# The opening of a three-block network on one core: four modulation groups as direct matmuls

## The reference, cut to what matters

```
mod = silu(c) @ ada_w[0] + ada_b[0]          # c: 1024, ada_w[0]: 1024 x 9216
sh1, sc1, g1, ... = split(mod, 9)            # 1024 each
h = rms_norm(x) * norm_g * (1 + sc1) + sh1   # the first layer's norm
x = x + 0.5 * g1 * swiglu(h, ff_w13, ff_w2)
...
m = rms_norm(mem, norm_mem_2[i])             # i = 0, 1: 256 memory tokens
mk, mv = split(m @ w_mem_kv_2[i], 2)         # 256 columns of keys, 256 of values
mk = rms_norm over each head of 64           # (inside the attention)
```

## Time and profile before

| | |
|---|---|
| median of 3 runs | 3224.15 us (3220.56 to 3226.03) |
| profiled execution | 3219.94 us, its span 3218.1 us |
| mean granted clock of TensorE | 0.968 |
| busy: TensorE, VectorE, ScalarE | 95%, 72%, 53% |
| the opening (up to the `wide` step) | 0 to 87.3 us |

### The profile page before, as it was taken

The page is one execution under the profiler, slowest core; times in us unless marked ns, Lnnn a source line. Parts: engine busy times, 40 slices in busy tenths (PEclk is TensorE's granted clock), DMA queues, the critical chain, the costliest instruction groups (busy, mean ns, idle before and its releaser), DMA issues.

```text
span 3218.1 us, 48507 instructions
## 1 busy us (share of the span) xinstructions
PE 3061.1 (95%) x20774; PEld 2819.0 (88%) x20774; DVE 2316.6 (72%) x2612; ACT 1700.4 (53%) x1902; POOL 84.2 (3%) x163
## 2 busy tenths in 40 slices
PE   5999899999988999899979999999999999889999
PEld 5999799999988998799968888888887888889999
DVE  6786668788555556655575888898898888646575
ACT  3434443443534335443535777777777777445453
POOL 1010001011000000000000000000000000000000
PEclk9999899999989999999988999999999999989999
DMA  7685458688421653245413999999999999423353
GB/s 278 248 309 213 151 192 295 234 292 309 158 73 66 223 205 130 79 157 184 158 40 120 365 349 343 366 355 350 351 349 363 341 358 363 166 103 134 116 187 118
DMA packets 112316, 739.27 MB, mean 230 GB/s; under 512 B 12480, under 2 KB 12480, under 8 KB 32096
## 3 DMA queue, kind: packets, MB, share of 16 engines
q1 hardware_dynamic: 89424, 651.21, 54.3%
q0 software_dynamic: 22672, 84.91, 7.4%
HBM read 735.01 MB, written 1.05 MB: 229 GB/s over the span
## 4 chain that ended last, share of the span: by engine, by line
PE 74%; DVE 8%; ACT 3%; DMA 2%; issue 1%; DVEq 0%; ACTq 0%; POOLq 0%
PE ps L521 54%; PE ps L520 18%; DVE wlo L2701 3%; PE ps L530 2%; DMA ring<-in_w 2%; DVE AF L2683 2%; ACT whi L1814 2%; DVE att L2692 0%; DVE gf L2686 0%; DVE AF L2674 0%; DVE hl L2674 0%; ACT cv L1802 0%; DVE gs L2689 0%; DVE T L2674 0%; DVE X L2674 0%
## 5 line engine op out<-in xcount | busy, mean ns | idle before, releaser
L2701 DVE TENSOR_TENSOR wlo<-ring,whi 128x2048 fp32r<-128x2048 f32 x620 | 1416.6, 2290 | 444.3 <-ACT whi L1814 443.4
L1814 ACT ACTIVATE whi<-ring 128x2048 fp32r<-128x2048 f32 x620 | 1185.0, 1914 | 350.9 <-issue 202.3
L521 PE MATMUL ps<-whi,AR 128*128 128x512 f32 (+1 forms) x2724 | 881.2, 398 | 0.7 <-DVE AR L2674 0.4
L521 PE MATMUL ps<-hh,whi 128*128 128x256 f32 x2464 | 696.3, 283 | 4.0 <-DVE wlo L2701 3.6
L521 PE MATMUL ps<-hl,whi 128*128 128x256 f32 x2464 | 689.4, 280 | 0.0
L521 PE MATMUL ps<-hh,wlo 128*128 128x256 f32 x2464 | 688.9, 280 | 0.0
L521 PEld LDWEIGHTS ps<-whi,AR 128*128 128x128 f32 x2724 | 511.0, 188 | 116.1 <-DVE AF L2674 1.1
L521 PE MATMUL ps<-wlo,AR 128*128 128x512 f32 (+1 forms) x1362 | 535.2, 393 | 0.0
L521 PEld LDWEIGHTS ps<-hh,whi 128*128 128x128 f32 x2464 | 463.6, 188 | 9.4 <-DVE wlo L2701 3.8
L521 PEld LDWEIGHTS ps<-hl,whi 128*128 128x128 f32 x2464 | 463.5, 188 | 1.2 <-issue 1.0
L521 PEld LDWEIGHTS ps<-hh,wlo 128*128 128x128 f32 x2464 | 463.2, 188 | 0.3
(11 more groups left out here) (234 smaller groups left out, 3238.1 us busy)
## 6 DMA issues: line engine op xcount, KB each, us to landing
ring<-in_w SPq DMA_DIRECT2D x620, 1024.0 KB, 5.2
rring<-in_r POOLq DMA_DIRECT2D x151, 512.0 KB, 5.0
AF<-in_mem POOLq DMA_DIRECT2D x2, 1024.0 KB, 5.9
X<-in_x POOLq DMA_DIRECT2D x1, 1024.0 KB, 13.6
AF<-in_cst POOLq DMA_DIRECT2D x1, 1024.0 KB, 5.7
y_out<-X SPq DMA_DIRECT2D x1, 1024.0 KB, 3.9
cst<-in_cst POOLq DMA_DIRECT2D x1, 672.5 KB, 4.7
sm<-in_small POOLq DMA_DIRECT2D x1, 378.0 KB, 4.9
```

Source lines behind the costliest of these rows:

```text
L521: return self.e.matmul(out, l, r, start=start, stop=stop)
L1814: self.e.activation(N.whi[:, c % HB, :], N.ring[:, c % RING, :], ACT.Copy).then_inc(N.sem["hi"], 1)
L2701: self.e.tensor_tensor(N.wlo[:, c % HB, :], N.ring[:, c % RING, :], N.whi[:, c % HB, :].bitcast(F32), ALU.subtract).then_inc(N.sem["lo"], 1)
```

## The change

- TensorE's new `direct(g, q)` multiplies a raw chunk by `ca`: the weights are its 128x128 blocks, the moving operand one column, 8 calls a chunk, and the four columns of a group add up in PSUM. `HEAD` gives the order: groups 2, 3, 0, 1. VectorE only adds the bias (`ada_sums` for g < 4, `part_sums`).
- The memory's norm factor is no longer multiplied in ahead of the products. `upper` and `lower` work on the memory as it was loaded (`s_xm`), with the gain only. The values get the factor as the scale of their copy out of PSUM (`copy_nat`), and the key norm takes care of it by a bias of 1e-6 times the memory's mean square plus 1e-6 squared (`ms`, `key_root`), since the keys are normed again. The memory's `spread` goes.
- The second memory has tiles of its own (`s_mh2`, `s_ml2`), so `hh` and `hl` are free, and the first layer's norm is applied inside `memory`.
- Loads: GpSimd issues small, three raw chunks, mem, cst, x, where it was cst, small, mem, three raw chunks, x. SP waits for x, not for mem, and sends weight chunks 1, 2 and 3 only when raw chunks 5, 8 and 11 have been used.
- The engines' orders in `memory` are rewritten: on TensorE eight raw chunks, both stats, four, the spread, four, then both layers' keys, then the values; `start` of TensorE and VectorE doesn't wait for cst, and ScalarE makes its small tables later (`tables`).

```diff
         assert ar.n <= free
+        ar = Arena(self.AR)
+        self.s_ml2, self.s_mh2 = ar.take(8, S), ar.take(8, S)
...
-                (self.scale if (key, "n") == FIRST else self.norm)((key, "n"), self.N.X, ("mod", l, 2 * j))
+                if (key, "n") != FIRST:
+                    self.norm((key, "n"), self.N.X, ("mod", l, 2 * j))
...
+HEAD = [(g, q) for g in (2, 3, 0, 1) for q in range(4)]
...
     def start(self):
-        self.wait_ge("ld_cst", 16)
-        self.wait_ge("ld_small", 16)
         self.wait_ge("dve", "ones")
         self.wait_ge("act", "consts")
...
+    def direct(self, g, q):
+
+        l, j = divmod(g, 18)
+        b = self.take(("ada", g)) if q == 0 else self.ps(("ada", g))
+        i, c = self.raw([(0, "ada_w", (l,), q * 256, 2, (j * 512, 512))])
+        for k in range(2):
+            w = self.N.ca[:, 2 * q + k:2 * q + k + 1]
+            for m in range(4):
+                o = k * 512 + m * P
+                t = self.mm(b[:, m:m + 1], c[:, o:o + P], w, q == 0 and k == 0 and m == 0, q == 3 and k == 1, skip=True)
+        t.then_inc(*self.up(("raw", i), *([("ada", g)] if q == 3 else [])))
+
     def memory(self):
 
 
         N = self.N
         self.base, self.span = 0, 7
-        for g in range(4):
-            self.ada(g, 0)
-            self.ada(g, 1)
         self.adan = 4
+        for g, q in HEAD[:8]:
+            self.direct(g, q)
         self.stat("mem", [N.s_tm[:, k, :] for k in range(8)])
-        self.spread("mem")
         self.stat(FIRST, [N.T[:, k, :] for k in range(8)])
+        for g, q in HEAD[8:12]:
+            self.direct(g, q)
+        self.wait_ge("ld_cst", 16)
+        self.wait_ge("act", "tables")
         self.spread(FIRST, 7)
-        self.ada_sums(0)
-
-        def lin(i, hh, hl):
+        for g, q in HEAD[12:]:
+            self.direct(g, q)
+        halves = ((N.s_mh, N.s_ml), (N.s_mh2, N.s_ml2))
+        for i, (hh, hl) in enumerate(halves):
             self.lin(("mem", i, "k"), [(0, "w_mem_kv_2", (i,), 0, 8, (0, 256))], ("mem", i), hh=hh, hl=hl)
-
-        def nat(i, hh, hl):
-            self.lin_nat(("mem", i, "v"), [(0, "w_mem_kv_2", (i,), 0, 8, (256, 256))], ("mem", i), hh=hh, hl=hl)
-
-        lin(0, N.s_mh, N.s_ml)
-        nat(0, N.s_mh, N.s_ml)
         self.pair_stat("mk0")
-        self.ada_sums(1)
-        lin(1, N.hh, N.hl)
+        nats = [self.nat_steps(("mem", i, "v"), [(0, "w_mem_kv_2", (i,), 0, 8, (256, 256))], ("mem", i), hh=hh, hl=hl)
+                for i, (hh, hl) in enumerate(halves)]
+        next(nats[0])
         self.pair_rows("mk0")
-        nat(1, N.hh, N.hl)
-        self.mark(("mem", 1, "in"))
+        self.pair_stat("mk1")
+        next(nats[0])
         self.pair_bcast("mk0")
-        self.ada_sums(2)
-        self.pair_stat("mk1")
-        self.ada_sums(3)
         self.pair_rows("mk1")
+        next(nats[1])
         self.pair_bcast("mk1")
+        next(nats[1])
+        self.mark(("stfree", self.row["mem"]))
...
     def start(self):
         N = self.N
+        self.wait_ge("dve", "ones")
+        self.act(N.misc[:, 62:63], N.ones[:, 0:1], ACT.Silu)
+        self.wait_ge("ld_small", 16)
+        self.act(N.ca[:, :], N.V("c", 0), ACT.Silu, "consts")
+        self.loaded = self.here()
+
+    def tables(self):
+        N = self.N
         self.wait_ge("ld_cst", 16)
         self.act(N.identb[:, :], N.C("ident"), ACT.Copy)
         self.act(N.maskb[:, :], N.C("mask"), ACT.Copy)
-        self.act(N.warm[:, :], N.C("iota")[:, 0:P], ACT.Copy)
-        self.wait_ge("ld_small", 16)
-        self.act(N.ca[:, :], N.V("c", 0), ACT.Silu, "consts")
-        self.wait_ge("act", "consts")
+        self.act(N.warm[:, :], N.C("iota")[:, 0:P], ACT.Copy, "tables")
 
     loaded = 0
...
-    def copy_nat(self, key, dst, wid=256):
+    def copy_nat(self, key, dst, wid=256, scale=None):
         for tb in range(2):
             self.wait_ge("mm", (key, tb))
-            self.act(dst(tb), self.ps((key, tb))[:, 0:wid], ACT.Copy, (*key, tb), ("free", (key, tb)))
+            kw = {} if scale is None else {"scale": scale[:, tb:tb + 1]}
+            self.act(dst(tb), self.ps((key, tb))[:, 0:wid], ACT.Copy, (*key, tb), ("free", (key, tb)), **kw)
 
...
     def memory(self):
         N = self.N
         self.adan = 4
-        self.squares("mem", N.s_xm, 8, lambda k: self.wait_ge("ld_mem", 16), N.s_tm)
-        self.squares(FIRST, N.X, 8, lambda k: self.wait_ge("ld_x", 16), N.T)
-        self.root("mem", 1024)
+        ms = N.misc[:, 34:36]
 
         def upper(i, hh):
             gain = N.V("norm_mem_2", i)
             for k in range(8):
-                self.wait_ge("dve", ("mem", "z", k))
-                self.act(hh[:, k, :], N.s_tm[:, k, :], ACT.Copy, (("mem", i), "hi", k), scale=gain[:, k:k + 1])
+                self.act(hh[:, k, :], N.s_xm[:, k, :], ACT.Copy, (("mem", i), "hi", k), scale=gain[:, k:k + 1])
 
         def keys(i):
             self.copy_out(("mem", i, "k"), N.m_mk[i])
             self.pair_squares(f"mk{i}", N.m_mk[i], "act", ("mem", i, "k"))
-            self.copy_nat(("mem", i, "v"), lambda tb: N.m_mv[i][:, tb, :])
-
-        self.split_to(1)
+
+        def key_root(i):
+            key = f"mk{i}"
+            st = N.st[:, self.take_row(key), :]
+            self.wait_ge("mm", (key, "ss"))
+            ss = self.ps((key, "ss"))
+            self.act(st[:, 0:4], ss[:, 0:4], ACT.Sqrt, scale=1.0 / 64, bias=ms[:, 0:1])
+            self.act(st[:, 4:8], ss[:, 4:8], ACT.Sqrt, (key, "sqrt"), ("free", (key, "ss")), scale=1.0 / 64, bias=ms[:, 1:2])
+
+        def values(i):
+            self.wait_ge("dve", ("mem", "rstd"))
+            self.copy_nat(("mem", i, "v"), lambda tb: N.m_mv[i][:, tb, :], scale=N.st[:, self.row["mem"], :])
+
+        self.wait_ge("ld_mem", 16)
         upper(0, N.s_mh)
+        self.squares("mem", N.s_xm, 8, lambda k: None, N.s_tm)
+        self.squares(FIRST, N.X, 8, lambda k: self.wait_ge("ld_x", 16), N.T)
+        self.tables()
+        self.wait_ge("mm", ("mem", "ss"))
+        self.act(ms, self.ps(("mem", "ss"))[:, 0:2], ACT.Identity, ("mem", "ms"), scale=EPS / 1024, bias=N.C("eps2"))
+        self.root("mem", 1024)
+        self.split_to(0)
         self.root(FIRST, 1024)
-        upper(1, N.hh)
+        upper(1, N.s_mh2)
+        self.split_to(2)
+        self.wait_ge("dve", ("part", 0, 0))
+        self.halves(FIRST, N.T, N.hh, 8, gain_of(N, ("mod", 0, 0))[1])
         self.split_to(3)
+        self.wait_ge("act", ("mem", "ms"))
         keys(0)
-        self.root("mk0", 64, 4)
+        self.split_to(4)
+        keys(1)
+        key_root(0)
         self.rows_out("mk0", 4)
         self.split_to(5)
-        keys(1)
-        self.root("mk1", 64, 4)
+        key_root(1)
         self.rows_out("mk1", 4)
-        self.wait_ge("mm", ("mem", 1, "in"))
+        values(0)
+        values(1)
...
         self.e.memset(self.N.rT[1][:, :], 0.0).then_inc(*self.up("zeros"))
-        self.wait_ge("ld_cst", 16)
         self.wait_ge("ld_small", 16)
...
             if k >= 2:
                 self.lower(key, N.T, N.hl, N.hh, (k - 2,), shift)
-        if key == FIRST:
-            self.pair("mk1", N.m_mk[1], N.V("g_mk_2", 1))
 
...
         cols = N.mod[:, l, m]
+        if g < 4:
+            self.tt(cols, self.ps(("ada", g))[:, 0:4], N.V("ada_b", l)[:, m], ALU.add, ("free", ("ada", g)))
+            if j % 2:
+                self.part_sums(l, part)
+            return
         turned = self.ps(("ada", g)).rearrange("p (a b) -> p a b", a=4)
         self.e.tensor_reduce(out=cols, in_=turned, axis=AX, op=ALU.add).then_inc(*self.up(("free", ("ada", g))))
         self.wait_ge("dve", self.here())
         self.tt(cols, cols, N.V("ada_b", l)[:, m], ALU.add)
         if j % 2:
-            self.wait_ge("dve", self.here())
-            mm = N.mod[:, l, part * 8:part * 8 + 8]
-            if part % 3 == 1:
-                self.stt(N.gain[:, l, part // 3, :], mm, 1.0, N.V("norm_g", l, part // 3), ALU.add, ALU.mult)
-            elif part in (2, 8):
-                self.ts(mm, mm, 0.5, None, ALU.mult, None)
-            self.mark(("part", l, part))
+            self.part_sums(l, part)
+
+    def part_sums(self, l, part):
+        N = self.N
+        self.wait_ge("dve", self.here())
+        mm = N.mod[:, l, part * 8:part * 8 + 8]
+        if part % 3 == 1:
+            self.stt(N.gain[:, l, part // 3, :], mm, 1.0, N.V("norm_g", l, part // 3), ALU.add, ALU.mult)
+        elif part in (2, 8):
+            self.ts(mm, mm, 0.5, None, ALU.mult, None)
+        self.mark(("part", l, part))
 
...
             gain = N.V("norm_mem_2", i)
             for k in range(8):
                 self.wait_ge("act", (("mem", i), "hi", k))
-                self.stt(hl[:, k, :], N.s_tm[:, k, :], gain[:, k:k + 1], hh[:, k, :].bitcast(F32), ALU.mult, ALU.subtract,
+                self.stt(hl[:, k, :], N.s_xm[:, k, :], gain[:, k:k + 1], hh[:, k, :].bitcast(F32), ALU.mult, ALU.subtract,
                          (("mem", i), "h", k))
 
```

(54 more changed lines are left out.)

## The result

The changed kernel takes 3242.41 us (median of 5 runs, 3238.38 to 3244.24), the kernel before 3220.56 in the same rounds: ratio 1.0064 [1.0049 to 1.0078], so 0.64% slower. The forecast was 3247, 3242.7 for the profiled execution; that one took 3242.41 around a span of 3240.6, which is 22.5 longer than before, where 22.8 were forecast. The 3247 was 22.8 on top of 3224.15, the median of the kernel before over three runs; its median over all five is 3220.56, and that difference of 3.6 is most of the 4.6 by which 3242.41 lies under it. The sum for the span came out, though two of its terms and one of its assumptions did not.

A forecast was written before the change was run, and what follows sets the result against it. TensorE's queue was taken to bound the changed opening: 105.7 us, plus 5.0 waits and 1.0 clock, put the gate at 111.7, 24.4 later. Less 1.6 at the wide step, that is 22.8 us slower: 3247 us, range 3235 to 3258.

The forecast's parts named there:

- Where it counts: Opening: the change is worth what it moves the gate, the first feed-forward layer's first matmul, plus the clock right behind.
- Its own signs of being wrong: Changed profile: new records spaced near 0.11, TensorE holes ending with a raw landing, or a changed time behind the gate.
- Price of a record: New one-column products on TensorE in the opening: 0.215 us a record at the lower clock, 55.0 us in all.
- Rival 1: Clock rises in the new products: 0.11 us a record, raws bind, gate at 81.7, 7.2 us faster, 3217; chance 0.11.
- Start: TensorE's first work, needing only the small table and raw chunk 0: at 6.5 us.
- Raw waits: TensorE's waits for raw chunks in the opening: 0.5 us for raw 3, 0 for later ones.
- Rival 3: Raws come late: TensorE waits 2.5 us more for each third chunk, 11 in all, 3258; chance 0.06.
- Keys and values: TensorE behind the products: 96 key matmuls 14.0 us, starting at the lower clock; both value products 11.3.
- Waits at the key norms: TensorE's holes before the gate: 3.1 us at pair_rows mk1, 0.9 before the second values, 0.5 before the wide step.
- Clock behind them: Second values behind the key-norm holes: if the clock falls, half run at the lower level, 2.3 us; 1.0 taken.
- Wide step: 96 matmuls from the gate on: warm at 11.4 us where they took 13.0, 1.6 back.
- Everything behind as now: Rest of the kernel behind the wide step: unchanged, but 23 us later.

The follow-up runs named there:

- e1: Changed kernel with the products of all four groups back on VectorE, rest of the new order nearly unchanged; 3218.66 us, ratio 0.9989 to the kernel before.
- e9: Changed kernel with 24 dense matmuls of 256 columns ahead of each raw chunk's products, into a free bank; 3261.25 us, ratio 1.0118 to the kernel before.
- e3: Changed kernel with 8 dense 256-column matmuls ahead of each raw chunk's products and 14 more ahead of the first; 3262.12 us, ratio 1.0126.
- e8: Changed kernel with only 28 of the 128 direct calls, loads, order and waits kept; 3225.82 us, ratio 1.0014 to the kernel before.
- e7: Changed kernel with SP waiting for mem, not x, and sending weight chunks 0 to 3 at once; 3242.82 us, ratio 1.0063 to the kernel before.
- e4: Changed kernel with the direct product's operands swapped: one ca column as weights, 512 raw columns moving; 3237.16 us, ratio 1.0045.
- e5: From e1: memory's keys and values ahead of the first layer's norm, key norms' rows later, weight chunks behind raws; 3195.23 us, ratio 0.9912.
- e2: Changed kernel with both inverse roots before the keys' scaling and first values copied out earlier, closing TensorE's key-norm holes; 3234.98 us, ratio 1.0043.

## Why the prediction held, and where it did not

- *Where it counts.* Right: the opening's chain ran along VectorE and runs along TensorE now, and the span followed the gate. Over these eleven kernels the stretch from gate to end is 3118.4 to 3132.7 us while the gate moves by 67.
- *Its own signs of being wrong.* Of the three that it named, two came, both small: holes that end with a raw landing (3.0 us), and a time behind the gate that changes too (some 4 us).
- *Price of a record, 0.215.* Right: 256 in 55.5 us (55.0 in the sum), at the lower level throughout. e1 shows that they are the cost (3242.4 against 3218.7), e9 that they would cost about half at the upper level. The Trainium skill, "TensorE: Matmul & The Clock Gate", Part 1, says that the default is throttled and that activity releases it; here one-column products from 6 to 35 us, with holes of 1.17 and 0.50 alone, did not release it, and e3 shows it falling with TensorE never idle.
- *Rival 1's price.* Its condition did not occur, and its time was too low: it had put the gate at 81.7 with the raws as the bound, while e8, with 22% of the calls and so cheaper products than the upper level would give, has it at 98.4. The sum had 29.9 us for the 13 raws from raw 3 on and 3 for the part of the stats that does not overlap them. In e8 the last 12 alone, from raw 3 (17.8) to raw 15 (63.3), take 45.5, with the stats' 13.7 in it: while TensorE is at the stats it frees no place in the ring. An estimate, from rows of e8, of what the upper level would still have given it: the two stats at half, -7, and the keys -1.4 (12.7 us against 96 x 0.118), so a gate near 90, beside 87.3 before. The change would then have been about as fast as before, and the 0.09 on the faster side leaned on a gate that the raws don't allow.
- *Start.* 6.5 forecast, 6.01 measured.
- *Raw waits.* The term that failed: 0.5 was put down for raw 3 and nothing for the others, by the argument that a window of 6.9 us from issue to use would do. Measured 1.17 + 0.50 + 1.03 + 0.31 = 3.0. The argument took the queue to be less crowded, with the weight chunks going out one by one. But raw 5 was issued (16.67) right behind weight chunk 0 (16.24) and was there 8.4 us later, and raws 14 and 15 stood beside three weight chunks at once (8.4 and 8.0 us, see e7). Raw 3 landed at 17.5, not 17, and was wanted 0.4 earlier than forecast. Sending the weights early does not end the waits: it makes them 4.2. Rival 3, raws that come late, was thus real, at 3.0 us and not its 11.
- *Keys and values.* 96 matmuls from 78.76 to 92.47, 13.7 us; 14.0 forecast.
- *Waits at the key norms.* 2.89, 0.91 and 0.66 against 3.1, 0.9 and 0.5: right. *Clock behind them:* I took 1.0, as about a half chance of 2.3; the whole 2.3 came (24 matmuls in 5.17 us). It was no bad luck: the same two holes stand in e1, e3, e4, e7, e8 and e9, and the clock fell in or behind them each time (0.50 to 0.64 over the matmuls that follow). Start -0.5, raws +2.5, clock +1.3 and keys -0.3 make +3.0 of the 3.8 by which the gate missed 111.7. Of the last 0.8, 0.5 are the tails of the short matmuls in front of the three holes, which the sum had under other work, and 0.3 is the second pair_bcast, which began at the lower level.
- *Wide step.* 11.3 against 13.0, 1.7 back; 1.6 forecast.
- *"Everything behind as now."* Not right. The gate is 28.2 later, the end of the wide step 26.5, and the end of the kernel 22.5. The first matmul behind the first layer's output, which stood at 418.73, is at 442.48, 23.75 later. Windows of the stretch between, of the kernel after:
```profile
226.50:306.50 80.00, 78.97 (x673) 78.64 (x672) 67.84 (x76) 31.69 (x26) 9.53 (x18) 1.00 0.87 315
305.00:384.00 79.00, 70.86 (x537) 67.95 (x536) 49.62 (x79) 40.70 (x63) 1.60 (x3) 0.94 0.39 143
```
In the kernel before the clock of the second stretch (280 to 360) is 0.89. 0.11 x 80 = 8.8 against 0.06 x 79 = 4.7 us of full-speed time are lost, an estimate of 4 us that came back where the code is the same. The starts of single matmuls give less for this stretch, 26.5 - 23.75 = 2.7, and 1.3 further on. Why the clock falls in other places there was not tried, and with one profile of each kernel this can't be told from scatter: executions of the kernel before alone run from 3212.1 us (mean clock 0.969) to 3236.4 (0.963). So the forecast of the span (+22.8 against +22.5) owes its precision to luck, two misses of opposite sign, +3.8 at the gate and -4 behind it; that the change costs some 20 us was not luck. The likeliest one's own range of 3239 to 3253 was the honest statement, though its upper end is added up short: with the waits doubled and all 48 of the second values' matmuls at the lower level its terms give a gate of 105.7 + 10.0 + 4.6 = 120.3, not 117, and 3255.

What stays open: the clock between 300 and 400 us, and the 6.3 us that e5 wins behind its gate.

## What to carry to other kernels

Work moved to an engine that is idle in the opening is paid at that engine's price of the opening: one-column f32 products cost twice there what they cost amid dense work, and they do nothing to raise the clock. Before moving work off an engine, look at the order in which the queues take it. With the products left on VectorE a better order, together with the norm factor at the copy, brought the gate 18.9 us forward (e5); the change as it was made took it 28.2 back, 17 of that for the products (e8) and 11 for its order. And when a change brings both an order and a move, run the order by itself first; it was not good here either (e8), and only e1's waits showed the line that was wrong.

## What the hardware showed that I had not expected

- The granted clock falls while TensorE has no idle time: 0.50 for 92.5 us in e3, with 8 dense records of 256 columns behind every 16 of one column. With 24 it stayed at 1.00 through the products (e9).
- A product with one weight column and 512 moving ones costs 1.88 us per chunk at best and does the work of 16 records of 0.214 (e4).
- Behind the gate, where the work is the same, these kernels' profiled executions differ by up to 14 us, and executions of one kernel by 24; the slowest and the fastest of the kernel before have mean granted clocks of 0.963 and 0.969. What moves the clock there was not tried.
- Two holes of TensorE of 2.9 and 0.9 us with two short matmuls between them: in all seven kernels that have them the clock fell, in four (after, e3, e7, e9) before the first matmul behind them, in three (e1, e4, e8) about 1 us into those matmuls. In e2, which closes the holes, it stayed at 1.00 from 98.4 to 107.
